# Two-layer backbone on one core: convolved channels first in layer 0's input projection, 16 modulation pieces beside it

## The chip, the core and the metric

One core of a Trainium2 chip runs the whole program. The time is the device time of one execution in microseconds (us); lower is better.

## The reference, cut to what matters

Layer 0 works on 256 latent and 256 context tokens (D = 1024). What the change touches:

```
m  = split(silu(c)     @ ada_w[l] + ada_b[l], 6)      # l = 0, 1: the modulation of both layers
mc = split(silu(c_ctx) @ ada_w[l] + ada_b[l], 6)
h  = rmsnorm(x) * (1 + m[1]) + m[0]                   # the same for the context with mc
nq, nk, nv, dq, dk, dv, dz, dg = split(h @ w_in)      # 7 x 512 columns and 16 gates
o_a = neighbourhood_attention(nq, nk, nv, ctx_k, ctx_v, rpb)
q, k, v = split(silu(conv5(concat(dq, dk, dv))))      # 5 taps along the tokens, 1536 channels
q = q / sqrt(sum(q*q) + eps) * 128**-0.5 ;  k = k / sqrt(sum(k*k) + eps)      # per head of 128
o_b = bidirectional_gated_delta(q, k, v, gates(dg))
```

Behind it come the output projection, a dense SwiGLU, and layer 1 with eight experts. The change leaves these alone; they use the later parts of m and mc.

## The kernel before, in words

The program is a row of blocks. In a block each engine has its own instruction list, and waits are on semaphores; a barrier stands between blocks. One big SBUF tensor, `arena`, holds most data at word offsets (`cut(offset, ...)`).

**Modulation in pieces.** `ada_w` of two layers is 6 groups of 2048 columns (`GROUPS`); a group is 8 pieces of 128 x 2048 fp32, 1 MiB each. `ada_product` (line 206) multiplies a piece by both conditioning vectors into bank 7: four products of 32 output rows each. Group 0 is made in the first block. The other 40 pieces come through `RING`, three places in `gate_rows`: `ada_load_slot` (line 193, SP) waits until the piece three before it is used (`s_au`), then loads; `ada_slot` (TensorE) waits for its landing and multiplies. After the eighth piece VectorE adds the bias (`ada_stage_rows`, line 227), TensorE turns the rows (`ada_turn`, line 219), VectorE makes columns (`ada_cols`), and SP stores gate rows and loads the next bias. All 40 run in the attention, `ada_slots_at` giving 0 to 2 pieces to each of its 32 jobs.

**Input projection** (block at line 711). 14 chunks of 256 columns of `w_in`, in order of columns: chunks 0 and 1 are queries, 2 and 3 keys, 4 and 5 values of the attention, 6 to 11 the 12 groups of 128 channels that are convolved, 12 and 13 the gate z. Three buffers; SP loads chunk c when chunk c - 3 is multiplied (`s_pj`). Weights are split into a high part (ScalarE, line 130) and a low part (VectorE, line 134), and each product is three matmuls (lines 139 to 141). A chunk is two output tiles of 8 x 3 matmuls of 512 columns (values: four tiles of 256 columns); ScalarE copies one tile out, VectorE the other (lines 767, 769). The 16 gates come last.

**Neighbourhood attention** (block at line 572). 32 jobs (8 heads by 4 tiles of tokens), the 16 of the context first. A context job is small: scores of 256 keys (line 595), two transposes (line 604), two products with the values (line 614). A latent job is large: 512 keys (lines 592 and 593, with the bias), four and four. Each job passes maximum (VectorE), exponent (ScalarE), normalising (VectorE), transposing, copying and multiplying, staggered over four jobs. Beside it POOL loads and masks the bias (line 918) and convolves channel groups 0 to 3; VectorE convolves groups 4 to 11, five passes each (lines 831 and 834), and makes the gates; behind the jobs ScalarE applies silu (line 839), VectorE squares (line 928), TensorE sums (line 933).

**Norm block** (line 960). The sums are copied, turned (line 975), get eps and a power (POOL, line 990); the factors are spread over partitions by 64 small products (line 982) and multiplied in.

Of the kernel before, what the change touches and what calls it, by code (L numbers as in the profile page):

```python
# [24 lines left out]
P = 128  # L25
# [3 lines left out]
T = 4  # L29
# [20 lines left out]
def build(nc, t, out):  # L50
    with ExitStack() as ctx:
# [177 lines left out]
        def ada_cols(dve, n):  # L229
# [12 lines left out]
            if g in GATES:  # L242
                dve.tensor_tensor(stage[:, :], stage[:, :], anorm[:, :], ALU.mult).then_inc(s_mg, 1)

        n_group_jobs = 6
        ada_slots_at = {n_group_jobs * n + d: [KD * n + s for s in ss]
                        for n in range(len(GROUPS) - 1) for d, ss in enumerate(((0, 1), (2, 3), (4, 5), (6,), (7,)))}

        def ada_pe_beside(pe, it):
            for m in ada_slots_at.get(it, ()):  # L250
                ada_slot(pe, m)
            n, d = divmod(it, n_group_jobs)
            if d == n_group_jobs - 1 and n + 1 < len(GROUPS):
                ada_turn(pe, n + 1)

        def ada_dve_beside(dve, it):
            n, d = divmod(it, n_group_jobs)
            if n + 1 < len(GROUPS):
                if d == n_group_jobs - 2:
                    ada_stage_rows(dve, n + 1)  # L260
                elif d == n_group_jobs - 1:
                    ada_cols(dve, n + 1)

        def ada_sp_beside(sp):
            for m in range(3, n_deferred):
                ada_load_slot(sp, m)
                n, k = divmod(m - 2, KD)
                if k == KD - 1:
                    ada_store_gates(sp, n + 1)
                    if n + 2 < len(GROUPS):  # L270
                        sp.wait_ge(s_ast, n + 2)
                        ada_load_bias(sp, n + 2)
            ada_store_gates(sp, len(GROUPS) - 1)
# [4 lines left out]
        WR = [cut(16384 + i * 4096, KD, 256) for i in range(NWR)]  # L278
        WRH = [cut(18432 + i * 4096, KD, 256) for i in range(NWR)]
# [3 lines left out]
        def load_in(sp, c):  # L283
            sp.dma_start(WR[c % NWR], WIN[:, :, c * 256:c * 256 + 256]).then_inc(s_wi0[c % NWR], 16)

# [7 lines left out]
        with nc.Block() as block:  # L293
            @block.sync
            def _(sp):
# [15 lines left out]
                for c in range(NWR):  # L311
                    load_in(sp, c)
# [254 lines left out]
        def attention(tag, jobs, qT, kT_of, v_of, bias_of, sink_of, prob, probT, pool_beside, act_beside, act_after, dve_beside, bias_ready=None, dve_after=None, pe_after=None, pe_beside=None, sp_beside=None):  # L567
# [131 lines left out]
        CX = cut(8192, 12, 2, 260)  # L699
# [6 lines left out]
            ("in_product", "in_copied_act", "in_copied_dve", "nat_bias_in", "in_w_high", "in_w_low"))  # L706


        in_jobs = [(c, m) for c in range(WCH) for m in range(4 if c in (4, 5) else 2)]
        made = [sum(cc <= c for cc, _ in in_jobs) for c in range(WCH)]  # L710
        with nc.Block() as block:
            @block.sync
            def _(sp):
                ada_load_bias(sp, 1)
                for c in range(NWR, WCH):
                    sp.wait_ge(s_pj, made[c - NWR])
                    load_in(sp, c)
                for m in range(3):
                    ada_load_slot(sp, m)

            @block.gpsimd
            def _(pool):
                pool.memset(CX[:, :, :, 0:2], 0.0)
                pool.memset(CX[:, :, :, 258:260], 0.0)

            @block.tensor
            def _(pe):
                for j, (c, m) in enumerate(in_jobs):
                    s = c % NWR
                    if m == 0:  # L730
                        pe.wait_ge(s_il, c + 1)
# [10 lines left out]
                pe.wait_ge(s_il, WCH + 1)  # L742
                for g in range(2):
# [5 lines left out]
            def evacuate(eng, parity, s_done, c):  # L749
                for j, (cc, m) in enumerate(in_jobs):  # L750
                    if cc != c or j % 2 != parity:
                        continue
                    eng.wait_ge(s_pj, j + 1)
                    b, scale = bank[j % 6][:, :], 1.0
# [18 lines left out]
            def _(act):  # L773
                def split(c):
                    if c < WCH:
                        act.wait_ge(s_wi[c % NWR], 16 * (c // NWR) + 16)
                        high(act, WRH[c % NWR], WR[c % NWR]).then_inc(s_ih, 1)
                    elif c == WCH:
                        act.wait_ge(s_wg, 16)
                        high(act, wgh, wg[:, :, :]).then_inc(s_ih, 1)  # L780
                split(0)
                split(1)
                for c in range(WCH):
                    evacuate(act, 0, s_pe_a, c)
                    split(c + 2)
# [5 lines left out]
            def _(dve):  # L791
                def split(c):
                    if c <= WCH:
                        dve.wait_ge(s_ih, c + 1)
                        v, hi = (WR[c % NWR], WRH[c % NWR]) if c < WCH else (wg[:, :, :], wgh)
                        low(dve, v, hi).then_inc(s_il, 1)
                split(0)
                split(1)
                for c in range(WCH):
                    evacuate(dve, 1, s_pe_v, c)  # L800
                    split(c + 2)
# [103 lines left out]
        FX = cut(14432, 12, NTOK)  # L905
        conv_pool, conv_dve, conv_act, s_conv = convolve("dn", 12, 4, CX, FX, DNCONV, cut(27232, 2, 512))
# [3 lines left out]
        def mask_and_convolve(pool):  # L910
# [8 lines left out]
            conv_pool(pool)  # L919


        sq = hT
        s_sq, s_ssp = sem("dn_squares"), sem("dn_norm_sums")

        def squares(dve):
            for c in range(8):
                dve.wait_ge(s_conv, c + 1)
                dve.tensor_tensor(sq[:, c, :], FX[:, c, :], FX[:, c, :], ALU.mult).then_inc(s_sq, 1)

        def sums(pe):  # L930
            for c in range(8):
# [1626 lines left out]
```

## Time and profile before

| | before |
|---|---|
| median of 3 runs (lowest, highest) | 2439.62 us (2438.5, 2443.61) |
| the profiled execution: its own time, its span | 2453.92 us, 2452.1 us |
| busy PE, DVE, ACT, POOL | 89%, 59%, 46%, 11% of the span |
| granted TensorE clock, mean | 0.939 |
| first block | 0 to 47 us |
| input projection | 47 to 219.7 us |
| attention, with silu, squares and sums behind it | 219.7 to 388.2 us |
| norm block | 388.2 to 406.4 us |
| DMA, whole program | 507.17 MB |

PE is TensorE, DVE VectorE, ACT ScalarE, POOL GpSimd and SP the engine that issues most DMAs. A time in the profile stands against the start of the span. The span holds the profiled execution's instructions; the 1.8 us around them are in its own time. The granted clock is TensorE's: 1.00 is 2.4 GHz and 0.50 is 1.2 GHz. The profile counts an fp32 product that isn't split as two matmuls (x8 for a piece's four).

### The profile page before, as it was taken

Reading aid. Unit: us, or ns where it says so; the run is one execution under the profiler, and the core shown is the slowest. Engines: PE = TensorE matmul, PEld = TensorE weight load, DVE = VectorE, ACT = ScalarE, POOL = GpSimd, SP = SyncE. Lnnn points to the kernel's source line nnn. Section 1 sums busy time; section 2 is a strip of 40 time slices with the busy share of each in tenths; the row PEclk is TensorE's granted clock in tenths of the full one; section 3 lists DMA queues with packets and bytes.
Section 4 is the critical chain, followed back from the end, with each engine's and each line's share of the span. In section 5 each row is a group of like instructions: output and inputs, shape, how many; then the busy total and the mean of one; then the engine's idle time right before and its main releaser. Section 6 shows DMA issues by size and latency. Waiting matters only on the chain. (4 is left out here: it accounts for less than half of the span.)

```text
span 2452.1 us, 27622 instructions
## 1 busy us (share of the span) xinstructions
PE 2191.3 (89%) x10974; PEld 1758.9 (72%) x10974; DVE 1445.2 (59%) x1401; ACT 1117.4 (46%) x1215; POOL 258.1 (11%) x227
## 2 busy tenths in 40 slices
PE   4998897999779999895988779999999999999994
PEld 2884345898657888785845668888877887888783
DVE  3223644544733222325275658888888888888884
ACT  3221223222222221224124457777777777777773
POOL 0002900324100000001062100000000000000001
PEclk8999898999889999997978879999999999999997
DMA  6234762000126632223100369999999999999994
GB/s 245 90 132 160 301 229 67 1 1 1 69 52 206 206 93 63 86 69 103 53 1 1 132 222 370 372 371 378 375 358 355 376 373 368 365 369 371 347 375 167
DMA packets 246377, 507.17 MB, mean 207 GB/s; under 512 B 11998, under 2 KB 80791, under 8 KB 239847
## 3 DMA queue, kind: packets, MB, share of 16 engines
q1 hardware_dynamic: 242791, 491.17, 56.1%
q0 software_dynamic: 3456, 14.16, 1.5%
q8 instruction: 95, 1.56, 0.3%
q14 instruction: 35, 0.29, 0.0%
HBM read 485.34 MB, written 19.96 MB: 206 GB/s over the span
## 5 line engine op out<-in xcount | busy, mean ns | idle before, releaser
L134 DVE TENSOR_TENSOR arena_r<-arena,arena_r 128x2048 fp32r<-128x2048 f32 (+2 forms) x450 | 921.0, 2060 | 309.8 <-ACT arena_r L130 308.8
L130 ACT ACTIVATE arena_r<-arena 128x2048 fp32r<-128x2048 f32 (+2 forms) x450 | 772.7, 1730 | 285.6 <-DMA arena<-in_moe_w 250.4
L2273 PE MATMUL bank<-arena_r,gate_rows_r 128*128 128x512 f32 x896 | 350.9, 392 | 0.0
L139 PE MATMUL bank<-hT_r,arena_r 128*128 128x512 f32 (+2 forms) x656 | 255.2, 389 | 37.0 <-DVE arena_r L134 37.0
L2271 PE MATMUL bank<-arena_r,arena_r 128*128 128x512 f32 x672 | 267.5, 398 | 0.3 <-DVE arena_r L134 0.2
L2272 PE MATMUL bank<-arena_r,arena_r 128*128 128x512 f32 x672 | 261.8, 390 | 0.0
L140 PE MATMUL bank<-catT_r,arena_r 128*128 128x512 f32 (+2 forms) x656 | 254.3, 388 | 0.0
L141 PE MATMUL bank<-hT_r,arena_r 128*128 128x512 f32 (+2 forms) x656 | 254.0, 387 | 0.0
L2302 PE MATMUL bank<-arena_r,hT_r 128*128 128x512 f32 x448 | 179.5, 401 | 21.4 <-DVE catT_r L2395 21.4
L2273 PEld LDWEIGHTS bank<-arena_r,gate_rows_r 128*128 128x128 f32 x896 | 169.2, 189 | 36.5
L2304 PE MATMUL bank<-arena_r,catT_r 128*128 128x512 f32 x448 | 175.9, 393 | 0.0
L2303 PE MATMUL bank<-arena_r,hT_r 128*128 128x512 f32 x448 | 175.8, 392 | 0.0
L139 PEld LDWEIGHTS bank<-hT_r,arena_r 128*128 128x128 f32 (+1 forms) x656 | 124.4, 190 | 63.2 <-DVE arena_r L134 37.7
L2271 PEld LDWEIGHTS bank<-arena_r,arena_r 128*128 128x128 f32 x672 | 126.4, 188 | 25.7 <-DVE arena_r L134 1.3
L2272 PEld LDWEIGHTS bank<-arena_r,arena_r 128*128 128x128 f32 x672 | 126.5, 188 | 24.7
L140 PEld LDWEIGHTS bank<-catT_r,arena_r 128*128 128x128 f32 (+1 forms) x656 | 124.5, 190 | 25.2
L141 PEld LDWEIGHTS bank<-hT_r,arena_r 128*128 128x128 f32 (+1 forms) x656 | 124.3, 189 | 25.5
L2302 PEld LDWEIGHTS bank<-arena_r,hT_r 128*128 128x128 f32 x448 | 84.8, 189 | 47.2 <-DVE catT_r L2395 30.3
L139 PE MATMUL bank<-arena_r,hT_r 128*128 128x512 f32 (+2 forms) x288 | 102.1, 355 | 14.7 <-DVE arena_r L134 14.7
L140 PE MATMUL bank<-arena_r,hT_r 128*128 128x512 f32 (+2 forms) x288 | 101.0, 351 | 0.0
L2304 PEld LDWEIGHTS bank<-arena_r,catT_r 128*128 128x128 f32 x448 | 84.7, 189 | 18.4
L1501 ACT ACTIVATE arena<-bank 128x512 f32<-128x512 f32 x22 | 13.2, 598 | 184.6 <-PE bank L141 184.6
(377 smaller groups left out, 3199.5 us busy)
## 6 DMA issues: line engine op xcount, KB each, us to landing
arena<-in_moe_w SPq DMA_DIRECT2D x336, 1024.0 KB, 6.3
gate_rows<-in_ada_w SPq DMA_DIRECT2D x40, 1024.0 KB, 7.2
arena<-in_ffn_w SPq DMA_DIRECT2D x44, 512.0 KB, 5.1
arena<-in_ev_w_in SPq DMA_DIRECT2D x14, 1024.0 KB, 5.3
arena<-in_ffn_w SPq DMA_DIRECT2D x11, 1024.0 KB, 4.9
arena<-in_od_w_in SPq DMA_DIRECT2D x9, 1024.0 KB, 5.3
arena<-in_ada_w SPq DMA_DIRECT2D x8, 1024.0 KB, 17.6
expert_rows_in<-ada_bias_rows SPq DMA_DIRECT2D x8, 1024.0 KB, 7.1
```

The lines of the kernel that those rows point to most:

```text
L130: return act.activation(rounded(hi), v, ACT.Copy)
L134: return dve.tensor_tensor(rounded(v), v, rounded(hi).bitcast(F32), ALU.subtract)
L139: pe.matmul(acc, xh_, wh_, start=start, stop=False)
L140: pe.matmul(acc, xh_, wl_, start=False, stop=False)
L141: return pe.matmul(acc, xl_, wh_, start=False, stop=stop)
L1501: act.activation(sl[:, n % 2, :], bank[n % 2][:, :], ACT.Silu).then_inc(s_sl, 1)
L2271: pe.matmul(out_bank, hi, wh[:, k, :], start=(kk == 0), stop=False)
L2272: pe.matmul(out_bank, hi, wl[:, k, :], start=False, stop=False)
L2273: mm = pe.matmul(out_bank, lo, wh[:, k, :], start=False, stop=(kk == KD - 1))
L2302: pe.matmul(bank[6 + half][:, :], hi, wh[:, j, o], start=st, stop=False)
L2303: pe.matmul(bank[6 + half][:, :], hi, wl[:, j, o], start=False, stop=False)
L2304: mm = pe.matmul(bank[6 + half][:, :], lo, wh[:, j, o], start=False, stop=sp_)
```

## The change

The chunks are taken in the order `ORDER`: convolved channels at positions 0 to 5, then keys, values, queries, z. VectorE convolves the pair of channel groups of a chunk right after it (all 12, POOL none), ScalarE applies silu a chunk later, POOL squares groups 0 to 7, TensorE sums them ahead of positions 3 to 6 and turns the sums ahead of position 10; POOL takes the power. The convolution now works in place of its input. Of the 40 pieces, 0 to 15 (groups 1 and 2) are multiplied in the projection, two ahead of each of positions 1, 2, 3, 4, 7, 8, 9 and 10 (`IN_SLOTS`); `IN_LOADS` says behind which position SP asks for each. Pieces 16 to 18 are loaded in the projection too; 16 to 39 are multiplied in the attention, one in each of eight jobs out of ten. The attention loses convolution, silu, squares and sums; the norm block keeps only the spreading. In the first block the third chunk buffer moves to the place of a piece of the first modulation group, and its load waits for that group's last product.

```diff
@@ the modulation beside other work @@
-        n_group_jobs = 6
-        ada_slots_at = {n_group_jobs * n + d: [KD * n + s for s in ss]
-                        for n in range(len(GROUPS) - 1) for d, ss in enumerate(((0, 1), (2, 3), (4, 5), (6,), (7,)))}
+        def ada_close_group(sp, n):
+            ada_store_gates(sp, n)
+            if n + 1 < len(GROUPS):
+                sp.wait_ge(s_ast, n + 1)
+                ada_load_bias(sp, n + 1)
+
+        IN_SLOTS = {p: (2 * i, 2 * i + 1) for i, p in enumerate((1, 2, 3, 4, 7, 8, 9, 10))}
+        IN_STAGE, IN_TURN = {5: 1, 11: 2}, {6: 1, 12: 2}
+        IN_LOADS = {1: (3, 4), 2: (5, 6), 3: (7,), 4: (8,), 5: (9, 10), 7: (11, 12), 8: (13, 14), 9: (15,), 10: (16,)}
+        n_group_jobs = 10
         def ada_pe_beside(pe, it):
-            for m in ada_slots_at.get(it, ()):
-                ada_slot(pe, m)
             n, d = divmod(it, n_group_jobs)
-            if d == n_group_jobs - 1 and n + 1 < len(GROUPS):
-                ada_turn(pe, n + 1)
+            if n < 3 and d < KD:
+                ada_slot(pe, KD * (n + 2) + d)
+            elif n < 3 and d == n_group_jobs - 1:
+                ada_turn(pe, n + 3)
...
+        ORDER = (6, 7, 8, 9, 10, 11, 2, 3, 4, 5, 0, 1, 12, 13)
@@ first block, SP @@
-                for c in range(NWR):
-                    load_in(sp, c)
+                for p in range(NWR):
+                    if p == 2:
+                        sp.wait_ge(s_au, KD)
+                    load_in(sp, p)
@@ projection, SP @@
                 ada_load_bias(sp, 1)
-                for c in range(NWR, WCH):
-                    sp.wait_ge(s_pj, made[c - NWR])
-                    load_in(sp, c)
                 for m in range(3):
                     ada_load_slot(sp, m)
+                for p in range(WCH - NWR):
+                    sp.wait_ge(s_pj, made[p])
+                    load_in(sp, p + NWR)
+                    for m in IN_LOADS.get(p, ()):
+                        ada_load_slot(sp, m)
+                    if p == 6:
+                        ada_close_group(sp, 1)
+                ada_load_slot(sp, 17)
+                ada_load_slot(sp, 18)
+                ada_close_group(sp, 2)
@@ projection, TensorE @@
-                for j, (c, m) in enumerate(in_jobs):
-                    s = c % NWR
+                for j, (p, m) in enumerate(in_jobs):
+                    s, c = p % NWR, ORDER[p]
                     if m == 0:
-                        pe.wait_ge(s_il, c + 1)
+                        if 3 <= p < 7:
+                            sums(p - 3)
+                        elif p == 10:
+                            turn_sums()
+                        for n in IN_SLOTS.get(p, ()):
+                            ada_slot(pe, n)
+                        if p in IN_TURN:
+                            ada_turn(pe, IN_TURN[p])
+                        pe.wait_ge(s_il, p + 1)
@@ projection, ScalarE and VectorE @@
+                for p in range(WCH):
+                    evacuate(act, 0, s_pe_a, p)
+                    split(p + 2)
+                    if 1 <= p <= PAIRS:
+                        conv_silu(p - 1)
...
+                    evacuate(dve, 1, s_pe_v, p)
+                    if p < PAIRS:
+                        convolve_pair(p)
+                    split(p + 2)
```

**SP in the projection.** `ada_w` rows are pieces, `ev_w_in` rows chunks. Before:

```order
L181 DMA ada_bias_rows<-in_ada_b 2x512 x4
L186 DMA ada_norm_rows<-in_norm_w 2x512 x2
L284 DMA arena<-in_ev_w_in 128x8x256 [waits in_product] x11
L193 DMA gate_rows<-in_ada_w 128x2048 x3
L711 UNCONDITIONAL_BRANCH
```

With the change:

```order
L186 DMA ada_norm_rows<-in_norm_w 2x512 x2
L193 DMA gate_rows<-in_ada_w 128x2048 x3
L289 DMA arena<-in_ev_w_in 128x8x256 [waits in_product] x2
L193 DMA gate_rows<-in_ada_w 128x2048 [waits ada_slot_used] x2
L289 DMA arena<-in_ev_w_in 128x8x256 [waits in_product]
L193 DMA gate_rows<-in_ada_w 128x2048 [waits ada_slot_used] x2
L289 DMA arena<-in_ev_w_in 128x8x256 [waits in_product]
L193 DMA gate_rows<-in_ada_w 128x2048 [waits ada_slot_used]
```

The first three pieces now go ahead of the chunks, and pieces 3 and 4 stand behind the second chunk load, the one that waits for positions 0 and 1 to be multiplied.

**TensorE between the second and the third chunk.** Before:

```order
L140 MATMUL bank<-catT_r_51,arena_r_54 128x512
L141 MATMUL bank<-hT_r_50,arena_r_54 128x512
L139 MATMUL bank<-hT_r_50,arena_r_54 128x512 [waits in_w_low]
L140 MATMUL bank<-catT_r_51,arena_r_54 128x512
L141 MATMUL bank<-hT_r_50,arena_r_54 128x512
```

With the change:

```order
L141 MATMUL bank<-hT_r_50,arena_r_54 128x512
L206 MATMUL bank<-gate_rows,small 32x512 [waits ada_ring2]
L206 MATMUL bank<-gate_rows,small 32x512 x3
L206 MATMUL bank<-gate_rows,small 32x512 [waits ada_ring0]
L206 MATMUL bank<-gate_rows,small 32x512 x3
L139 MATMUL bank<-hT_r_50,arena_r_53 128x512 [waits in_w_low]
```

Pieces 2 and 3 stand between the chunks; `ada_ring0` is the landing of piece 3, in the place that piece 0 left.

**TensorE from the last job to the spreading.** Before:

```order
L614 MATMUL bank<-arena 64x128 x3
L933 MATMUL bank<-hT,const 8x512 [waits dn_squares] x8
L572 UNCONDITIONAL_BRANCH
L971 UNCONDITIONAL_BRANCH [waits barrier_Pool_Activation_PE_DVE_SP_release]
L975 MATMUL bank<-const,small 128x8 [waits dn_norm_rows]
L975 MATMUL bank<-const,small 128x8 x3
L982 MATMUL bank<-const,small 128x128 [waits dn_rnorm]
```

With the change:

```order
L621 MATMUL bank<-arena 64x128 [waits nat_pv_copied,nat_turned_copied]
L621 MATMUL bank<-arena 64x128 x3
L579 UNCONDITIONAL_BRANCH
L1032 UNCONDITIONAL_BRANCH [waits barrier_Pool_Activation_PE_DVE_SP_release]
L1038 MATMUL bank<-const,small 128x128 x16
```

The spreading products follow on the barrier, with no sum, turn or power ahead of them.

## Rows read from the trace of the kernel before

**Rows 1.** Timeline of PE in the projection: start, us, what, [idle before].

```profile
51.23 0.80 PE L139 MATMUL bank<-hT_r,arena_r 128*128 128x512 f32 x1 [13.11 <-DVE arena_r L134]
...
56.28 0.40 PE L139 MATMUL bank<-hT_r,arena_r 128*128 128x512 f32 x1
...
218.03 0.39 PE L141 MATMUL bank<-hT_r,gate_weights_r 128*8 128x512 f32 x1
```

**Rows 2.** Windows: stretch, length, busy of each engine, granted clock, DMA share, GB/s.

```profile
180.00:200.00 20.00, 20.00 (x90) 16.57 (x89) 3.78 (x4) 3.20 (x4) 0.00 (x0) 1.00 0.34 140
...
235.00:237.00 2.00, 2.00 (x12) 0.37 (x12) 2.00 (x1) 0.62 (x3) 2.00 (x2) 0.53 0.83 270
237.00:239.00 2.00, 2.00 (x15) 0.83 (x8) 2.00 (x2) 0.00 (x0) 2.00 (x1) 1.00 0.97 324
```

**Rows 3.** Waits between 217 and 405 us: total, times, longest us.

```profile
PE bank L206 <- DMA gate_rows<-in_ada_w: 21.5, 13, 7.2
```

**Rows 4.** Timeline of PE in the attention.

```profile
219.81 0.67 PE L595 MATMUL bank<-arena 64*128 64x256 f32 x2 [1.40 <-PEq L711]
...
231.20 1.93 PE L206 MATMUL bank<-gate_rows,small 128*32 128x512 f32 x8 [7.24 <-DMA gate_rows<-in_ada_w]
...
265.49 0.70 PE L595 MATMUL bank<-arena 64*128 64x256 f32 x2
...
267.07 1.06 PE L206 MATMUL bank<-gate_rows,small 128*32 128x512 f32 x8
268.06 0.70 PE L595 MATMUL bank<-arena 64*128 64x256 f32 x2
...
363.89 1.12 PE L592 MATMUL bank<-arena 64*128 64x512 f32 x2
...
367.03 1.12 PE L592 MATMUL bank<-arena 64*128 64x512 f32 x2
...
370.17 0.65 PE L604 MATMUL bank<-const,arena 128*128 128x128 f32 x4
```

**Rows 5.** Timelines of DVE, ACT and PE behind the attention.

```profile
374.87 0.29 DVE L655 COPY catT<-bank 128x128 f32<-128x128 f32 x1 [2.33 <-PE bank L614]
...
376.93 6.35 ACT L839 ACTIVATE arena<-arena 128x512 f32<-128x512 f32 x12
...
395.58 9.86 PE L982 MATMUL bank<-const,small 128*128 128x128 f32 x64 [6.23 <-POOLq L993]
```

**Rows 6.** Instructions of lines 284 and 193 (SP's loads), with the time to landing.

```profile
L284 SPq DMA_DIRECT2D arena<-in_ev_w_in x11: 367/368/399, 64.6 to 174.7; - x11
...
DMA to landing us min/median/max: 5.1/5.3/5.8
...
L193 SPq DMA_DIRECT2D gate_rows<-in_ada_w x1: 352/352/352, 278.0 to 278.0; - x1
...
DMA to landing us min/median/max: 4.8/4.8/4.8
...
L193 SPq DMA_DIRECT2D gate_rows<-in_ada_w x2: 424/428/432, 278.4 to 278.9; - x2
...
DMA to landing us min/median/max: 6.9/7.9/8.9
```

**Rows 7.** Timeline of DVE, and its convolution passes as a group.

```profile
185.63 0.69 DVE L769 TENSOR_SCALAR arena<-bank 128x512 f32<-128x512 f32 x1 [7.99 <-PE bank L141]
186.24 2.28 DVE L134 TENSOR_TENSOR arena_r<-arena,arena_r 128x2048 fp32r<-128x2048 f32 x1
...
370.02 1.53 DVE L834 SCALAR_TENSOR_TENSOR arena<-arena,channel_cols 128x512 f32<-128x512 f32 x2
...
L834 DVE SCALAR_TENSOR_TENSOR arena<-arena,channel_cols 128x512 f32<-128x512 f32 x32 | 28.3, 884 | 0.3
```

**Rows 8.** Instructions of line 293, the barrier that ends the first block, in part.

```profile
L293 SPq COMPARE_BRANCH  x1: 33/33/33, 45.7 to 45.7; - x1
...
L293 SPq EVENT_SEMAPHORE  x1: 17/17/17, 46.8 to 46.8; - x1
```

More of the change, by code:

```diff
@@ L698, in build @@
         nqT, nkT, V, zT = cut(0, 4, NTOK), cut(2048, 4, NTOK), cut(4096, T, 512), cut(6144, 4, NTOK)
-        CX = cut(8192, 12, 2, 260)
+        CX = cut(14336, 12, 2, 260)
+        FX = cut(14336, 12, 520)[:, :, 0:NTOK]
+        conv_tmp, sq = cut(12288, 2, NTOK), cut(13312, 2, NTOK)
+        RL = small[:, 64:96]
         natb = cut(23136, 2, 8, 256)
@@ L706, in build @@
             ("in_product", "in_copied_act", "in_copied_dve", "nat_bias_in", "in_w_high", "in_w_low"))
-        in_jobs = [(c, m) for c in range(WCH) for m in range(4 if c in (4, 5) else 2)]
-        made = [sum(cc <= c for cc, _ in in_jobs) for c in range(WCH)]
+        s_pad = sem("conv_pads")
+        in_jobs = [(p, m) for p in range(WCH) for m in range(4 if ORDER[p] in (4, 5) else 2)]
+        made = [sum(pp <= p for pp, _ in in_jobs) for p in range(WCH)]
+        PAIRS = 6
+        s_cd, s_si, s_sq, s_ssp, s_srow, s_stu, s_sse, s_rl = (sem(f"dn_{x}") for x in
+            ("convolved", "conv_silu", "squares", "norm_sums", "norm_rows", "norm_rows_turned", "norm_sums_eps", "rnorm"))
         with nc.Block() as block:
@@ L773, in _, with split, conv_silu @@
             def _(act):
[L774 to L778, printed above, removed]
+                def split(p):
+                    if p < WCH:
+                        act.wait_ge(s_wi[p % NWR], 16 * (p // NWR) + 16)
+                        high(act, WRH[p % NWR], WR[p % NWR]).then_inc(s_ih, 1)
+                    elif p == WCH:
                         act.wait_ge(s_wg, 16)
                         high(act, wgh, wg[:, :, :]).then_inc(s_ih, 1)
+                def conv_silu(q):
+                    act.wait_ge(s_cd, 10 * q + 10)
+                    for m in range(2):
+                        act.activation(FX[:, 2 * q + m, :], conv_tmp[:, m, :], ACT.Silu).then_inc(s_si, 1)
                 split(0)
                 split(1)
-                for c in range(WCH):
-                    evacuate(act, 0, s_pe_a, c)
-                    split(c + 2)
+                for p in range(WCH):
[3 more added lines that the diff above has]
+                        conv_silu(p - 1)
+                    if p == 8:
+                        act.wait_ge(s_ssp, 8)
+                        act.activation(sq[0:8, 0, :], bank[6][0:8, :], ACT.Copy).then_inc(s_srow, 1)
                 act.wait_ge(s_pj, len(in_jobs) + 1)
@@ L918, in mask_and_convolve @@
                     pool.tensor_tensor(v, v, m, ALU.add).then_inc(s_ncol, 1)
[L919 to L931, printed above, removed]
-                pe.wait_ge(s_sq, c + 1)
-                mm = pe.matmul(bank[7][0:8, :], cst("eighth")[:, 7 - c:15 - c], sq[:, c, :], start=(c == 0), stop=(c == 7))
-            mm.then_inc(s_ssp, 1)
         nat_jobs = [(tile, c, part) for tile in (2, 3, 0, 1) for c in range(4) for part in range(2)]
```

125 lines of the change are left out of this document (70 added, 55 removed).

## The prediction

> **What bounds the kernel now.** I read TensorE's timeline and the stages by windows first, then its waits, since a change that only moves work can pay only where TensorE, the engine that all wait for here, stands still. The projection is full: from its first product at 51.23 to its last at 218.03 [rows 1] nothing on TensorE waits, and a window inside it shows PE busy for all of its 20 us at a granted clock of 1.00, so a 512-column product passes every 0.22 us, while the DMA engines are used to 0.34 [rows 2]. The attention is not full: it runs from 219.81 to 375.16 (374.87 + 0.29), 155.3 us, and in it TensorE waited 21.5 us for pieces of the modulation weights, 7.24 us at one place [rows 3 to 5]. After it comes a tail in which TensorE is almost idle: from 375.16 to the first spreading product at 395.58, 20.4 us go to silu of 12 channel groups, 8 squares, 8 sums, a turn and a power [rows 5]. So the change moves work out of two stages with holes into one without any. Whatever it adds to TensorE there costs its full length, and so does every wait that it brings with it.
>
> **Added to the projection: work.**
> - 16 pieces. A piece at the full clock takes 267.07 to 268.06 = 0.99 us [rows 4]: 16 x 0.99 = 15.8.
> - 8 sums of squares. Each is a plain fp32 product of 512 columns; the two of that width at 363.89 take 1.12 together with their split into two passes, so one product costs 1.1 [rows 4]: 8.8.
> - Two turns of 0.65, the price of four transposes of that size [rows 4], and four small transposes, some 0.4 (estimate from a turn): 1.7.
> - Sum 26.3, all on the path.
>
> **Added to the projection: waits.** This is the term that decides. The ring has three places. SP issues the loads in program order, and the excerpt of its order shows that after chunk 1 is done it first loads a chunk of input weights and then piece 3; TensorE's order shows piece 3 asked for before chunk 2's first product, that is by the engine that has just finished chunk 1. The load starts when it is needed. The same holds at positions 3 (piece 5), 4 (7), 8 (11), 9 (13) and 10 (15); at 1 and 7 both pieces were asked for earlier. How late is it? A chunk of input weights lands 5.3 us after its issue. Three pieces issued together at 278.0, 278.4 and 278.9 landed after 4.8, 6.9 and 8.9 us, one every 2.5 us, the first not held up by those behind it [rows 6]. So a piece behind a chunk lands about 5.3 + 2.5 + 0.1 = 7.9 us after the chunk's end. Ahead of it TensorE has only the other piece (0.99), at positions 3 and 4 also two sums (2.2), at 10 the small turn (0.4). Waits: 3 x 6.9 + 2 x 4.7 + 6.5 = 36.6 us.
>
> The Trainium skill, "DMA: Bandwidth & Descriptors", section "Anatomy of one DMA", fits a DMA as about 2.0 us plus its bytes at 436 GB/s, which makes 4.4 us for 1 MiB and 6.8 for two in a row. By that estimate each of the six waits is 1.1 us shorter and the kernel takes 2449. The trace has 4.8 us for a piece alone and 5.3 for a chunk [rows 6], both above the page's 4.4; I keep the rows.
>
> Each wait also costs clock. Behind the wait of 7.24 us that ended at 231.20 the granted clock was still 0.53 from 235 to 237 and 1.00 only after that; the piece behind the wait took 1.93 instead of 1.06 [rows 2, 4]. At the projection's start, 12 products took 56.28 - 51.23 = 5.05 us instead of 2.7, a loss of 2.3 [rows 1]; after the 7.24 us wait about 5.6 us ran at half clock, a loss of 2.8. I take 2.5 at each of the six places: 15. The bounds are 0 (the clock does not fall in the two waits of 4.7) and 3.
>
> **Hidden in the projection.** VectorE's convolution of a pair is 10 passes of about 0.75 (two take 1.53), beside a copy of 0.7 and a split of 2.28: 10.5 us per chunk. A chunk lasts 10.9: the 7.99 for which VectorE waits ahead of the copy, the copy and the split [rows 7]. That fits, barely; the cover is the chunk. ScalarE's silu (6.35 / 12 = 0.53 each [rows 5]) and POOL's squares have most of a chunk free. Chunk loads are issued three chunks ahead and stay hidden.
>
> **First block.** SP now waits for the last product of the first modulation group before the third chunk load, ahead of seven small loads whose arrival closes the block. SP got there at 45.7, about 1.0 ahead of the barrier that opens at 46.8 [rows 8]. Half to two us more on SP leave a cost of 0 to 1; I take 1.
>
> **Taken from the attention.** By TensorE's own work it needs: 16 small jobs of 1.58 (265.49 to 267.07), 16 large ones of 3.14 (363.89 to 367.03) [rows 4], 24 pieces of 0.99, 3 turns of 0.65, less 2.5 for the first jobs that have nothing to turn yet, plus the 5.0 in which the last jobs drain: 25.3 + 50.2 + 23.8 + 2.0 - 2.5 + 5.0 = 103.8. The same sum with 40 pieces and five turns gives 121 for before, and the other 34 us were the 21.5 of waits, half clock behind them, and jobs slowed by VectorE. What stays of these: the fourth piece still cannot be asked for before the first is used, and the bias matrix of 2 MB still travels beside it, so it lands again 11.4 us after the start (231.20 - 219.81) while TensorE gets there at 6.7: 4.7 of wait, 2.5 of clock, and 2 for smaller ones. With one piece per job, and none in two jobs of ten, later loads have three jobs (7.7 us and more) to arrive. So 113, a gain of 42.3; bounds 36 and 48.
>
> **Taken from the tail.** Silu, squares, sums, turn and power are gone, and the sigmoid and a barrier stay, some 1.9 of the 20.4: gain 18.5. The 64 spreading products (9.86 us [rows 5]) start on a warmer engine: 2 more.
>
> **Sum.** +26.3 + 36.6 + 15 + 1 - 42.3 - 18.5 - 2 = **+16.1 us**, slower. The profiled execution took 2453.92, span 2452.1; it would be 2470. It is 14.3 above the median of the three runs, and the differences carry over: 2439.6 + 16.1 = 2456. A measurement of this kernel can tell 0.2%, 5 us, from no change.
>
> **Rivals.**
> - *The waits are not there* (faster). Should the piece be copied beside the chunk rather than behind it, or the chunk load be short, it would land near the 4.8 to 5.3 of a load alone. The waits then shrink by 2.6 each, and the two shortest no longer cost clock; waits plus clock fall from 51.6 below 35.5, and the kernel turns faster. It decides at a landing about 5.2 us behind the chunk's end. With no wait at all it is 2456 - 51.6 = 2404. For it: SP's queue is asynchronous, and the engines are at a third of their use. Against: the three pieces of [rows 6] came one after another. 10%.
> - *Waits at the short end.* Landing at 6.8, clock lost at only the three or four long places: 30 + 8 instead of 51.6, so 2442, no change. 8%.
> - *VectorE becomes the bound of the projection.* With POOL busy beside it a convolution pass took 0.88 on the mean [rows 7], which makes 11.8 of a chunk's 10.9; three of the six chunks have a wait to hide it. POOL's two squares can stretch a split too. 3 to 5 chunks late by 1 to 3 us: 2456 + 10 = 2466. The Trainium skill, "GPSIMD Engine Reference", section "Specifications", says that GpSimd shares its SBUF interfaces with VectorE where the latter has two SBUF inputs, as the convolution and the split do; the 0.88 against 0.75 agrees. 12%.
> - *The attention does not shrink so.* If its jobs are held by the chain of maximum, exponent and normalising rather than by TensorE, only the 16 pieces and half of the waits go (26): 2472. Against: at 265.49 jobs pass at TensorE's rate. 8%.
>
> **Chances and range.** Forecast 62%, rivals 10, 8, 12 and 8. Slower 0.82, within 0.2% 0.08, faster 0.10. The forecast's own bounds: clock 9 to 18, landing 6.8 to 8.9, attention 36 to 48. Low end 2438 takes in the second rival, high end 2471 the third; the first is left out.
>
> **What the profile will show.** If right: in the projection six waits of TensorE for pieces, 4 to 7.5 us each, behind chunks 1, 2, 3, 7, 8 and 9, each followed by products of 0.43 instead of 0.22 us; a projection of some 245 us from first to last product; an attention of 113 with one wait of some 5 us near its start; spreading products within 2 us of its end. It is wrong if the projection has no such waits (piece copied early), if TensorE there waits for the splits (VectorE the bound), or if the attention stays above 125.

## The result, and the profile after

Over 7 runs each the changed kernel took 2457.27 us in the median (2455.88 to 2470.95), the kernel before 2443.54 (2438.5 to 2451.24): a ratio of 1.0071 with an interval of [1.0042, 1.01]. It is slower by 13.7 us; the sum said 16.1 on a median of 2439.6. Two of the changed kernel's seven runs, 2470.65 and 2470.95 at a mean granted clock of 0.934 and 0.935, stand apart from the other five (2455.88 to 2458.92, 0.941 to 0.944), and neither of them was profiled.

The page of the changed kernel begins like this (part 1, and the clock of part 2):

```profile
span 2454.1 us, 27622 instructions
...
PE 2185.6 (89%) x10974; PEld 1753.8 (71%) x10974; DVE 1448.8 (59%) x1413; ACT 1116.1 (45%) x1214; POOL 203.8 (8%) x199
...
PEclk8898999999889999997978879999999999999997
```

Its profiled execution took 2455.88, span 2454.1. That is only 2.0 above the span of the profiled execution of before, so the stages have to be set side by side. The projection is first. Timeline of PE, its first two and its last product (start, us, what, [idle before]):

```profile
51.06 0.79 PE L139 MATMUL bank<-hT_r,arena_r 128*128 128x512 f32 x1 [13.11 <-DVE arena_r L134]
...
296.78 0.39 PE L141 MATMUL bank<-hT_r,gate_weights_r 128*8 128x512 f32 x1
```

It lasts from 51.06 to 297.17, 246.1 us where before it was 167.2 [rows 1]. In it stand six waits for pieces of modulation weights, here one of them with the piece ahead of it, and all six by the view of waits (total, times, longest):

```profile
77.65 1.06 PE L206 MATMUL bank<-gate_rows,small 128*32 128x512 f32 x8
86.16 1.93 PE L206 MATMUL bank<-gate_rows,small 128*32 128x512 f32 x8 [7.45 <-DMA gate_rows<-in_ada_w]
...
PE bank L206 <- DMA gate_rows<-in_ada_w: 38.4, 6, 7.4
```

The piece behind the wait, at 86.16, took 1.93 us; the one ahead of it, at 77.65, took 1.06: the clock had fallen. The load that it waited for was issued half a microsecond after the chunk's end, right behind the load of a chunk of input weights. Instructions of lines 289 and 193 (count: shortest, median and longest in ns, first and last start in us), with the time from issue to landing:

```profile
L289 SPq DMA_DIRECT2D arena<-in_ev_w_in x1: 373/373/373, 77.8 to 77.8; - x1
...
DMA to landing us min/median/max: 5.2/5.2/5.2
...
L193 SPq DMA_DIRECT2D gate_rows<-in_ada_w x1: 579/579/579, 78.2 to 78.2; - x1
...
DMA to landing us min/median/max: 7.9/7.9/7.9
```

The chunk lands 5.2 us after its issue at 77.8, the piece 7.9 after its issue at 78.2, at 86.1, where TensorE's wait ends. The five others landed 7.2 to 7.6 after theirs. Windows of 20 us show the clock (stretch, length, busy us of PE, PEld, DVE, ACT, POOL, granted clock, DMA share, GB/s):

```profile
80.00:100.00 20.00, 13.84 (x57) 9.75 (x58) 7.11 (x10) 3.44 (x4) 0.00 (x0) 0.83 0.38 148
100.00:120.00 20.00, 14.85 (x57) 9.10 (x56) 10.57 (x12) 2.80 (x3) 2.39 (x2) 0.83 0.43 159
160.00:180.00 20.00, 20.00 (x94) 14.80 (x93) 10.42 (x13) 4.63 (x6) 0.00 (x0) 1.00 0.54 198
180.00:200.00 20.00, 13.24 (x80) 9.55 (x79) 2.89 (x2) 1.59 (x2) 0.00 (x0) 0.83 0.43 158
```

Where no piece comes late (160 to 180) PE is busy for all 20 us at 1.00. Elsewhere it stands for up to 7 us and runs a part of the rest at 0.5. DVE is busy for 3 to 11 us of 20: it is not what PE waits for. Its convolution of a pair is the group at 100.83 and the one behind it (timeline of DVE):

```profile
100.83 1.67 DVE L870 TENSOR_SCALAR arena<-arena,channel_cols 128x512 f32<-128x512 f32 x2 [0.20 <-DVE arena L820]
102.42 6.16 DVE L873 SCALAR_TENSOR_TENSOR arena<-arena,channel_cols 128x512 f32<-128x512 f32 x8
108.50 2.28 DVE L134 TENSOR_TENSOR arena_r<-arena,arena_r 128x2048 fp32r<-128x2048 f32 x1
```

Eight passes in 6.16 are 0.77 each, and the split of 2.28 follows at once.

Then the attention and its end (timelines of PE and DVE):

```profile
298.56 0.67 PE L602 MATMUL bank<-arena 64*128 64x256 f32 x2 [1.39 <-PEq L725]
...
310.88 1.94 PE L206 MATMUL bank<-gate_rows,small 128*32 128x512 f32 x8 [5.47 <-DMA gate_rows<-in_ada_w]
...
410.97 0.29 DVE L662 COPY catT<-bank 128x128 f32<-128x128 f32 x1 [2.07 <-PE bank L621]
...
412.02 7.38 PE L1038 MATMUL bank<-const,small 128*128 128x128 f32 x64 [1.09 <-PEq L579]
420.45 0.63 PE L1063 MATMUL bank<-const,catT 8*128 8x8 f32 x8 [1.04 <-PEq L1025]
```

The attention lasts from 298.56 to 411.26, 112.7 us (155.3 before), the spreading follows 0.8 later (20.4 before [rows 5]) and takes 7.38 for 64 products (9.86 before). The product behind the spreading comes 369.4 us after the projection's first one; before, at 406.48, it came 355.3 after. So in the changed stages the kernel lost 14.1 us, what the medians say too.

The missing 12 of the two profiled spans lie where no line was changed. The last of four barriers of one line lies ahead of layer 1's experts (count: ns, first to last start in us), first before, then after:

```profile
L572 POOLq EVENT_SEMAPHORE  x4: 17/17/17, 388.1 to 1317.1; - x4
```

```profile
L579 POOLq EVENT_SEMAPHORE  x4: 17/17/17, 411.8 to 1331.3; - x4
```

Up to it the lead of before is still 14.2 us (1317.1 against 1331.3). Behind it the experts' matrices are read, and there the profiled execution of before was the slower one. Windows of 200 us (columns as above), before and after:

```profile
1700.00:1900.00 200.00, 194.19 (x873) 158.95 (x872) 167.99 (x94) 146.46 (x108) 1.34 (x3) 0.99 1.00 364
```

```profile
1700.00:1900.00 200.00, 196.65 (x889) 161.03 (x888) 173.26 (x96) 149.55 (x108) 1.60 (x3) 1.00 1.02 372
```

The DMA engines are full in both, and moved 364 and 372 GB/s. The profiled execution of before took 2453.92, more than any of the seven timed runs (median 2443.54). A difference of two profiled spans is thus no measure here; the stages and the medians are.

### The profile page after: what moved, and what is told of

The parts are those of the page before. It is cut to its first block and busy times, and to the rows that moved or that the text cites. A ratio compares the mean times of both kernels' runs of the same rounds, so it can differ in the third digit from the quotient of the medians.

```text
span 2454.1 us, 27622 instructions
## 1 busy us (share of the span) xinstructions
PE 2185.6 (89%) x10974; PEld 1753.8 (71%) x10974; DVE 1448.8 (59%) x1413; ACT 1116.1 (45%) x1214; POOL 203.8 (8%) x199
## 5 line engine op out<-in xcount | busy, mean ns | idle before, releaser
L139 PE MATMUL bank<-hT_r,arena_r 128*128 128x512 f32 (+2 forms) x656 | 259.2, 395 | 37.3 <-DVE arena_r L134 37.3
L141 PE MATMUL bank<-hT_r,arena_r 128*128 128x512 f32 (+2 forms) x656 | 256.7, 391 | 0.0
L139 PE MATMUL bank<-arena_r,hT_r 128*128 128x512 f32 (+2 forms) x288 | 103.2, 358 | 14.6 <-DVE arena_r L134 14.6
L820 DVE TENSOR_SCALAR arena<-bank 128x512 f32<-128x512 f32 (+1 forms) x16 | 10.0, 625 | 151.3 <-PE bank L141 151.3
```

What stands on the lines that cost most here:

```text
L139: pe.matmul(acc, xh_, wh_, start=start, stop=False)
L141: return pe.matmul(acc, xl_, wh_, start=False, stop=stop)
L820: ins = eng.tensor_scalar(dst, b, scale, None, ALU.mult)
```

## The experiments

The theory: the second piece of a pair is requested by the very chunk that stands ahead of its use, behind another load, and so costs six waits with their half clock; this is what turns a gain into a loss. The rivals: the work added to TensorE and VectorE is itself too much for the projection (then early requests gain little), or the waits are only another face of a limit in the ring or the queue (then they come back elsewhere).

**Ask for the pieces one or two chunks earlier.** Nothing but the table of requests is changed, and the loads of pieces 17 and 18 move into it. A ring place is then still in use when SP asks for it, but not for long: in this kernel's trace the first piece of a pair is issued 1.0 to 2.7 us behind its chunk's load.

```diff
-        IN_LOADS = {1: (3, 4), 2: (5, 6), 3: (7,), 4: (8,), 5: (9, 10), 7: (11, 12), 8: (13, 14), 9: (15,), 10: (16,)}
+        IN_LOADS = {0: (3, 4), 1: (5, 6), 2: (7, 8), 3: (9, 10), 6: (11, 12), 7: (13, 14), 8: (15, 16), 9: (17, 18)}
...
-                ada_load_slot(sp, 17)
-                ada_load_slot(sp, 18)
```

> The change with each group of ring loads asked for one or two positions earlier (pieces 3 and 4 behind position 0, 5 and 6 behind 1, and so on), nothing else altered. Theory (the late requests cost the time: six waits of 38.4 us together and half clock behind each): no wait of TensorE for a piece in the projection, projection 246.1 -> about 195 us from first to last product, time 2457 -> 2405, that is some 35 below the kernel before. Rival (TensorE's added work or VectorE's convolution fills the projection, and would hold it where the waits do now): the waits change their releaser to the weight splits, projection above 215, time above 2425.

Measured: 2406.01 us (2403.36 to 2409.63), ratio to before 0.9835 [0.9812, 0.9858]. The same windows as above, and all waits for pieces from the projection's start to the spreading, of this kernel:

```profile
80.00:100.00 20.00, 20.00 (x101) 13.15 (x94) 15.89 (x22) 3.44 (x4) 2.39 (x2) 1.00 0.75 270
100.00:120.00 20.00, 20.00 (x92) 13.90 (x91) 14.22 (x16) 6.52 (x8) 2.39 (x2) 1.00 0.53 204
180.00:200.00 20.00, 20.00 (x136) 16.82 (x135) 3.15 (x4) 4.97 (x5) 5.70 (x2) 1.00 0.71 271
```

```profile
PE bank L206 <- DMA gate_rows<-in_ada_w: 5.5, 1, 5.5
```

PE is busy for all of each window at 1.00. The projection takes 195.0 (52.58 to 247.53): the added work is 195.0 - 167.2 = 27.8 us, and the waits and the clock of the change are 246.1 - 195.0 = 51.1, of which 38.4 are the waits and 12.7 the clock. TensorE's busy time says the same. The whole projection as one window (stretch, length, busy us of PE, clock, DMA share, GB/s), first in the change, then here:

```profile
51.06:297.17 246.11, 207.74 (x972) 0.91 0.35 127
```

```profile
52.58:247.53 194.95, 194.95 (x972) 0.99 0.44 161
```

The same 972 matmul records took 12.8 us longer in the change, and 38.4 us more it stood still. No wait came back elsewhere; the one left for a piece is that at the attention's start, 5.5 us here and in the change. DVE is busier in these windows (15.89 and 14.22 of 20) and still not waited for.

**Half of the early requests.** Only positions 2 to 4 are asked for early, so three waits must stay.

```diff
+        IN_LOADS = {0: (3, 4), 1: (5, 6), 2: (7, 8), 3: (9, 10), 7: (11, 12), 8: (13, 14), 9: (15,), 10: (16,)}
```

> The change with early requests for positions 2 to 4 only; those for 8 to 10 as late as in the change. Theory: three waits (7.4, 5.2 and 5.3 us) and their half clock go, three stay (6.8, 6.9, 6.8); projection 246 -> 221, time about 2432, in the middle between the change and the one with all requests early (2406). Rival (the waits move from the early positions to later ones): projection stays above 232.

Measured: 2432.81 (2426.75 to 2446.72), ratio 0.9964 [0.9946, 0.9982]. The projection takes 222.3, with waits of 6.73, 6.77 and 6.73. Less 195.0 and 20.2 that leaves 7.1 of half clock, 2.4 for each. So the three waits that were left kept their price when the other three went. One thing was off. The execution that was profiled took 2445.22, 12.4 above the median, and its attention 121.3 where the change's took 112.7, with the same code and the same two waits: one of 5.3 us (5.5 in the change) for a piece, and one of 1.9 for a copy by ScalarE (line 693). The second wait in the timeline of PE, and windows of PE ahead of it and behind it (columns as in the last view), in this kernel:

```profile
303.74 0.65 PE L621 MATMUL bank<-arena 128*64 128x128 f32 x4 [1.89 <-ACT arena L693]
```

```profile
298.00:302.00 4.00, 3.85 (x24) 0.98 0.64 213
...
306.00:310.00 4.00, 4.00 (x12) 0.50 0.00 1
...
318.00:322.00 4.00, 4.00 (x16) 0.50 0.79 262
```

The same in the change:

```profile
325.90 0.65 PE L621 MATMUL bank<-arena 128*64 128x128 f32 x4 [1.90 <-ACT arena L693]
```

```profile
318.00:322.00 4.00, 4.00 (x28) 0.97 0.88 287
...
326.00:330.00 4.00, 4.00 (x24) 1.00 0.32 133
```

Behind the first wait the clock was at a half for some 11 us in the one and some 7 in the other, and in both it was back at full ahead of the second. Behind the second it fell again here, to 0.50 until about 322 (17 us), and stayed at 1.00 in the change. Why one wait of 1.9 us costs the clock in one execution and not in another was not settled; it is one source of the spread between runs, and it comes back below.

**Keep the late requests, use the second piece later.** It is multiplied behind the first output tile of the chunk.

```diff
-                        for n in IN_SLOTS.get(p, ()):
+                        for n in IN_SLOTS.get(p, ())[:1]:
                             ada_slot(pe, n)
...
+                    elif m == 1:
+                        for n in IN_SLOTS.get(p, ())[1:]:
+                            ada_slot(pe, n)
```

> The change with its request times as they are, but the second piece of each pair multiplied in the middle of the chunk (between its two output tiles, 5.4 us later). Theory (a piece lands 7.9 us behind the end of the chunk before): waits shrink from 5.2 to 7.5 us each to 0 to 2.0, the clock stays at 1.00, time about 2412. Rival (the landing slides when TensorE works on, because chunk load and piece contend): waits stay above 4 us, time above 2435.

Measured: 2421.86 (2421.2 to 2429.92), ratio 0.9914 [0.9886, 0.9942]; the projection takes 213.2. Timeline of PE in it, the waits at positions 8 and 9:

```profile
173.64 1.59 PE L206 MATMUL bank<-gate_rows,small 128*32 128x512 f32 x8 [3.87 <-DMA gate_rows<-in_ada_w]
...
193.99 1.94 PE L206 MATMUL bank<-gate_rows,small 128*32 128x512 f32 x8 [4.90 <-DMA gate_rows<-in_ada_w]
```

At positions 2 and 10 the waits were 1.86 and 1.14, and at 3 and 4 there was none, as expected. At 8 and 9 the expectation missed, and with them the time, by 10 us, and the miss was mine: positions 8 and 9 are value chunks of four narrower tiles, so the second piece comes 2.9 us into the chunk and not 5. From a landing 7.9 after the chunk's end, less a piece of 1.0 and these 2.9, follow waits of 4.0; measured 3.87 and 4.90. The two pieces landed 8.0 and 9.0 us behind the end of the chunk before, where the change has 7.8 and 7.9 at these positions: the first stands where it was, the second came 1.1 later, and its chunk took 6.5 to land instead of 5.4. A slide by the whole shift of the use, as the rival had it, shows nowhere. The four waits, 11.8 us together, cost a further 6.4 of half clock (213.2 - 195.0 - 11.8).

**The convolution half alone.** Chunk order, convolution, squares and sums as in the change; all 40 pieces stay in the attention. Cut to its core:

```diff
+        ORDER = (6, 7, 8, 9, 10, 11, 2, 3, 4, 5, 0, 1, 12, 13)
...
+                        if 3 <= p < 7:
+                            sums(p - 3)
+                        elif p == 10:
+                            turn_sums()
...
+                    if p < PAIRS:
+                        convolve_pair(p)
...
-            conv_pool(pool)
```

> Only the convolution half of the change: new chunk order, convolution, silu, squares, sums and power in the projection, all 40 pieces back in the attention as before (0 to 2 per job). Theory: projection +9.2 (8 sums, small turn), tail behind the attention 20.4 -> about 1, spreading 2 less, attention 3 to 6 less with POOL and VectorE free of the convolution: 13 to 18 below the kernel before. Rival (VectorE late in the chunks): splits late, projection above 180, gain under 8.

Measured: 2430.32 (2426.08 to 2435.54), ratio 0.9932 [0.9906, 0.9959]. The projection takes 178.5 (+11.3 where 9.2 was expected) and has no waits; the spreading follows 0.8 us behind the attention. The attention takes 157.5 in the profiled execution (2435.54, 5.2 above the median), where 3 to 6 less than the 155.3 of before was expected:

```profile
PE bank L206 <- DMA gate_rows<-in_ada_w: 21.9, 11, 7.4
```

21.9 us of waits for pieces, where [rows 3] has 21.5: with VectorE and POOL relieved the attention is still held by its loads. The gain that shows is the tail's.

**The piece half alone**, with the early requests; old chunk order, convolution in the attention.

```diff
+        IN_LOADS = {0: (3, 4), 1: (5, 6), 2: (7, 8), 3: (9, 10), 6: (11, 12), 7: (13, 14), 8: (15, 16), 9: (17, 18)}
...
+                        for n in IN_SLOTS.get(c, ()):
+                            ada_slot(pe, n)
+                        if c in IN_TURN:
+                            ada_turn(pe, IN_TURN[c])
```

> Only the piece half, with the early requests: old chunk order, 16 pieces in the projection, convolution, silu and sums in and behind the attention as before. Theory: projection +17, attention 155 -> about 118, net 18 to 24 below the kernel before; with the convolution half the two gains add up to that of both (about 35). Rival (POOL's and VectorE's convolution, not the loads, hold the attention): attention stays above 128, gain under 12.

Measured: 2424.34 (2422.65 to 2426.03), ratio 0.9916 [0.9894, 0.9938]. The projection takes 185.2 (+18.0), the attention 118.2 (-37.1). The rival (an attention above 128, held by the convolution) is out. By the medians, beside the kernel before on the same chip (2444.95), the halves save 20.6 (pieces) and 14.6 (convolution), together 35.2, and both at once (the early requests above) save 38.9. By the stages of the profiled executions, from the projection's first product to the spreading's, or to the one behind it, they save 20.1 (pieces: 324.3 against 344.4) and 8.6 (convolution: 346.7 against 355.3), together 28.7, and both at once 35.3 (319.9 against 355.3); but the convolution half's profile is of a run 5.2 above its median. With some 6 us either way on each saving, the halves add up as far as these runs can tell. Whether taking the convolution out helps the attention is not shown: it cost 2.2 with 40 pieces there and saved 3.8 with 24 (118.2 to 114.4), both less than the 8.6 by which two executions of the same attention differed above.

**Late requests, but no half clock.** Ahead of each late piece TensorE multiplies something useless into the next free bank, sized to the wait. The products change no result; they only take its time.

```diff
+        FILL = {2: 31, 3: 21, 4: 22, 8: 28, 9: 29, 10: 28}
...
+                        for i, n in enumerate(IN_SLOTS.get(p, ())):
+                            if i and p in FILL:
+                                pe.wait_ge((s_pe_a, s_pe_v)[j % 2], (j - 6) // 2 + 1) if j >= 6 else None
+                                for f in range(FILL[p]):
+                                    pe.matmul(bank[j % 6][:, :], rounded(hT[:, f % KD, 0:P]), rounded(catT[:, f % KD, :]), start=True, stop=True)
                             ada_slot(pe, n)
```

> The change with TensorE kept busy while it waits for the late pieces: 21 to 31 useless products of 512 columns (0.227 us each, 4.8 to 7.0 us a place) ahead of each late piece, into a bank that the next chunk overwrites. The requests stay as late as they are. Theory (51.1 us of the projection's growth are 38.4 of waits and 12.7 of half clock behind them): the granted clock stays at 1.00, remaining waits below 1 us each, the projection 246 -> about 234, time about 2445. Rival (the half clock is no cost of its own, the rest of the growth comes from elsewhere, as late splits): projection and time stay within 3 us of the change's.

Measured: 2445.6 in 10 runs (2442.62 to 2453.18), ratio 1.0012 [0.9998, 1.0025]. Its windows:

```profile
80.00:100.00 20.00, 19.84 (x95) 14.83 (x87) 8.61 (x12) 3.43 (x4) 0.00 (x0) 1.00 0.42 158
100.00:120.00 20.00, 18.43 (x83) 12.39 (x83) 10.64 (x12) 3.44 (x4) 2.39 (x2) 1.00 0.42 159
180.00:200.00 20.00, 19.69 (x129) 15.91 (x129) 3.31 (x3) 0.73 (x3) 0.00 (x0) 1.00 0.42 158
```

The clock is 1.00 from 60 us to the projection's end, the DMA share is near that of the change, and the kernel is some 12 us faster than it (2445.6 against 2457.27; the kernel before had 2442.92 and 2443.54 beside them). The projection takes 237.2, 8.9 below the change's (about 234 was expected): PE is busy in it for 233.8, 38.9 above the early requests' 194.95 for 159 useless products (36.1 by the 0.227 of the expectation), and 3.4 us of waits are left, the longest 1.6. So the half clock behind the waits is a cost of its own, apart from the waits: 9 us were got back in the projection and 12 by the medians.

**The bias load behind the pieces.** What is left in the version with early requests is the wait at the attention's start, where the bias matrix of 2 MB travels beside the pieces. Here POOL asks for it only once piece 23 has landed (beside the early table).

```diff
+            pool.wait_ge(s_ring[23 % 3], 16 * (23 // 3) + 16)
             pool.dma_start(natb, t["nat_bias"]).then_inc(s_bias_in, 16)
```

> All requests early, and in the attention POOL asks for the 2 MB of bias only when piece 23 has landed, so that pieces 19 to 21 travel alone. Theory (the wait of 5.5 us at the fourth job, and the half clock until 272.8, come from the bias beside the pieces): that wait below 1 us, clock at 1.00, attention 114.4 -> about 104, time about 2395. Rival (the bias comes too late for the first large job, some 42 us after the start, since its load and mask take 15 to 20 us from then on): a wait for the mask of 3 us or more at the first large job, time 2402 or more.

Measured: 2404.3 (2398.46 to 2408.58), ratio 0.9851 [0.9827, 0.9876]: a miss, since 2395 was expected. The wait fell to 0.87, and the attention from 114.4 to 110.3, not to 104. The rival's time came, but not its mechanism: TensorE does not wait for the mask anywhere. What is left of the loss stands ten microseconds later. Timeline of PE, the windows there, and ACT's timeline ahead of it:

```profile
257.21 1.06 PE L206 MATMUL bank<-gate_rows,small 128*32 128x512 f32 x8 [0.87 <-DMA gate_rows<-in_ada_w]
...
266.31 0.65 PE L621 MATMUL bank<-arena 128*64 128x128 f32 x4 [1.89 <-ACT arena L693]
```

```profile
262.00:266.00 4.00, 2.41 (x16) 1.00 0.98 403
266.00:270.00 4.00, 3.69 (x16) 0.64 1.05 444
270.00:274.00 4.00, 4.00 (x14) 0.50 0.83 355
```

```profile
262.55 1.28 ACT L977 ACT_TABLE_LOAD   x1
...
264.49 1.28 ACT L978 ACT_TABLE_LOAD   x1
...
265.90 0.36 ACT L693 ACTIVATE arena<-bank 128x256 f32<-128x256 f32 x1
```

ScalarE does two gate activations (lines 977 and 978), each with a table load of 1.28, ahead of a copy that TensorE waits for. This is the wait of 1.9 us of the second experiment, and it was there all along: with early requests alone it stands at 278.30, also 1.89 us long, and the clock stayed at 1.00 behind it, in both executions. There the clock had been at a half behind the wait for a piece (0.50 in 260 to 272). Here that fall is gone, and the clock fell behind the short wait instead, to a half for some 13 us. TensorE's busy time in the attention hardly changed (106.5 and 107.2); only its waits did.

**And the gate rows later.** They are moved from the jobs 0 to 12 to the jobs 14 to 26, where the large jobs give ScalarE room (beside the two edits above).

```diff
-                  mask_bias, gates_act, gates_end,
-                  lambda dve, j: (gates_dve(dve, j), ada_dve_beside(dve, j)), bias_ready=(s_ncol, 4),
+                  mask_bias, lambda act, j: gates_act(act, j - 14), gates_end,
+                  lambda dve, j: (gates_dve(dve, j - 14) if j >= 14 else None, ada_dve_beside(dve, j)), bias_ready=(s_ncol, 4),
```

> As e6_bias, and the gate arithmetic that runs beside the attention's jobs 0 to 12 moved to jobs 14 to 26, where a job of TensorE is 3.1 to 4.1 us long. In e6_bias the two table loads of ScalarE at the seventh job (2.6 us) held a copy, TensorE waited 1.9 us for it, and behind it the clock was at half from 266.9 to about 280, which cost some 6 us. Theory (that short wait dropped the clock): no wait for the copy, clock at 1.00 through the attention, attention 110.3 -> 102 to 104, time 7 below e6_bias. Rival (the clock falls there because the small jobs give TensorE too little work, wait or not): the clock falls all the same within the small jobs, gain under 3 us.

Measured: 2400.16 (2398.84 to 2406.86), ratio 0.9823 [0.9802, 0.9844]. The attention takes 105.1 (248.87 to 353.95); its windows at the same places:

```profile
262.00:266.00 4.00, 4.00 (x27) 1.00 0.95 354
266.00:270.00 4.00, 3.71 (x24) 1.00 1.01 416
270.00:274.00 4.00, 4.00 (x26) 1.00 1.07 457
```

The clock is 1.00 on the mean of the whole attention, and TensorE stands still for 3.9 us of it, 1.2 at the longest. The rival (the small jobs themselves lower the clock) is out. That the clock stays because that wait has gone is likely and not more, as it had stayed with the wait in other executions. The two kernels it stands on were run again beside it. The one with the bias load behind the pieces:

> The kernel of e6_bias once more, beside e1_again and e8_gates on one chip, since its gain of 4 us against e1_early in the profile did not show in the medians of two chips (2404.3 and 2406.0). Theory: 3 to 5 us below e1_again. Rival: the delayed bias only moves the loss, 0 to 2 us.

Measured: 2405.16 (2400.95 to 2407.94), ratio 0.9833 [0.9812, 0.9854], the attention again 110.4, but made up otherwise: behind the same wait of 1.89 the clock was at a half for only some 3 us (0.97 on the mean of the attention, 0.94 the first time), but TensorE stood for 6.2 us in all (3.1). And the one with early requests alone:

> The kernel of e1_early once more, as the base for the two others of this call: 0.983 to 0.985 of the kernel before.

Measured: 2409.78 (2400.63 to 2415.65), ratio 0.985 [0.9822, 0.9877], the attention 114.3 (114.4 the first time). So in this set of runs the bias load is worth some 4 us and the gate rows 5 (7 were expected), both in the attention's length and in the medians, though the intervals of the ratios overlap and the first pair of medians differed by 1.7 only. The last version has the lowest median of all: 1.8% below the kernel before and 57 us below the change.

## Why the prediction was right

It said 2456, slower, by waits; it was 2457.27, and by those waits. By its own steps, each against the trace:

- **Added work**: 26.3 said, 27.8 measured (the early requests' projection against before's).
- **Waits**: 36.6 at six places said, 38.4 at six places measured. The pieces landed 7.8 to 8.4 us behind the chunk's end where 7.9 was said; SP issues the chunk's load 0.1 after that end and the piece's 0.5. The shorter landing of 6.8, estimated for two in a row from the fit of the Trainium skill ("DMA: Bandwidth & Descriptors", section "Anatomy of one DMA"), did not come: 7.2 to 7.9 from the pieces' own issue. The page gives that fit for DMAs that GpSimd issues, and these are SP's, which the prediction did not say.
- **Half clock**: 15 said, 12.7 measured here, 2.1 a place, and 2.4 a place where three were left. That the waits of about 5 us would cost it as well was right (0.83 in 100 to 120). TensorE's busy time and the run with useless products show this term apart from the waits.
- **First block**: 1 said, none: its barrier opened at 46.7, before at 46.8. The first product comes at 51.1 or 52.5 in different executions, with the same first block; a spread of 1.4 us that stage sums can't resolve.
- **VectorE in the projection**: hidden as said, with passes of 0.77. The rival that makes it the bound rested on 0.88 a pass, a mean from a stage where POOL was busy beside it; in the projection POOL is busy for 2.4 us of the 20 from 100 on, and in the attention of before for 73 of its 155.
- **Attention**: 42.3 said, 42.6 measured, with the wait of 5.47 near its start (4.7 said). Its floor of 103.8 by TensorE's own work holds as well: the last experiment, with 3.9 us of waits left, has 105.1. The part that the prediction gave to jobs slowed by VectorE is not shown: without the convolution TensorE stood for 23.7 us of the attention, and for 24.3 before.
- **Tail and spreading**: 18.5 and 2 said, 19.7 and 2.5 measured.

The sum of the measured terms is 27.8 + 38.4 + 12.7 - 42.6 - 19.7 - 2.5 = +14.1, what the ends of the stages give. What made it right was the step that asks who requests a load and when: read from the order of SP and the landing times of [rows 6], it tells a loss of 14 from a gain of 37 (2443.54 against 2406.01). The tests of it are the early requests, which took the six waits away and 51 us with them, and their half, which took three. The rival without waits, 2404, had the right price: the kernel with early requests took 2406. The landing at which it would turn faster was worked out less well: 5.2 holds with the full 15 of clock, and with the two shortest waits free of it, as the text has it, the turn comes at about 6.0; neither is near the 7.8 to 8.4 measured. Two pieces of luck have to be told. The terms that are 1.5 and 1.8 too small are made up by a clock term 2.3 too large and a first block 1 too large. And the sum was 2.4 above the measured difference of 13.7, while its base, the median of three runs, was 3.9 below the median of seven: the two errors made up for each other.

## What to carry to other kernels

In a stage where TensorE never stands still, work moved into it cost its full length here (27.8 us); moving paid for what it took out of a stage with holes, and only once its loads were asked for at least one step of the loop ahead of the one before their use. That was one line, the table of requests, and was worth 51 us.

Price a wait of TensorE as its length plus the half clock behind it, 2.1 to 2.4 us in dense products here. Amid the attention's small jobs that second part was anything from nothing to 17 us at half clock behind one and the same wait of 1.9 us, so there a single profile does not price it. When a wait is removed, look for the next one behind it: that for ScalarE's copy, 1.9 us long in each of these versions, took back a part of what putting off the bias load had gained.

## What the runs showed that was not expected

- The granted clock fell behind a wait of only 1.89 us amid the small jobs of the attention (0.64 and 0.50 for the next 8 us), while behind 7 us waits in the dense projection the whole loss was 2.1 to 2.4.
- It did not always fall there. The same wait of 1.9 us for the same copy left the clock at 1.00 in the change, in both executions with early requests and in two more, and brought it down in three: to 0.50 for 17 and for 13 us, and once for some 3. What decides it is open.
- Useless products during the waits made the kernel 9 to 12 us faster.
- Two profiled executions differed by 12 us in the experts' stage, whose code and data are the same.
